# Three homes of expert matrices that cycle to the end of the layer, in a two-layer encoder

## What is computed

```python
D_MODEL = 1024
MOE_EXPERTS = MOE_GROUPS * MOE_EXPERTS_PER_GROUP      # 4 * 8 = 32
MOE_TOP_K = 2
MOE_HIDDEN = D_MODEL // 2
...
    def expert_block(args):
        xb, e = args
        return (jax.nn.silu(xb @ w_gate[e]) * (xb @ w_up[e])) @ w_down[e]
...
    for layer in range(DEPTH):
        ...
        x = x + mix.astype(x.dtype)
        h = rms_norm(x, norm_ffn_g[layer])
        x = x + hier_moe(h, moe_w_group[layer], ..., moe_w_gate[layer], moe_w_up[layer], moe_w_down[layer])
    return rms_norm(x, norm_final_g)
```

## Time and profile before

| what | us, or as said |
|---|---|
| median of 3 runs | 1568.47 (1568.19 to 1569.04) |
| the profiled execution, time | 1564.83 |
| its span, first to last instruction | 1563.0 |
| PE busy / DVE / ACT / POOL | 1389.7 / 531.6 / 244.7 / 194.6 |
| matmuls / weight loads of PE | 7005 / 7005 |
| matrices' queue (q1), share of the 16 DMA engines | 71.9% |
| moved by all DMA engines | 479.25 MB, mean 307 GB/s |
| expert stage of layer 0, first to last gate-and-up product | 344.6 to 805.3 |
| expert stage of layer 1, the same | 1074.9 to 1532.6 |

### The profile page before, as it was taken

The page is one execution under the profiler, slowest core; times in us unless marked ns, Lnnn a source line. Parts: engine busy times, 40 slices in busy tenths (PEclk is TensorE's granted clock), DMA queues, the critical chain, the costliest instruction groups (busy, mean ns, idle before and its releaser), DMA issues. The chain is left out here.

```text
span 1563.0 us, 18994 instructions
## 1 busy us (share of the span) xinstructions
PE 1389.7 (89%) x7005; PEld 660.3 (42%) x7005; DVE 531.6 (34%) x1254; ACT 244.7 (16%) x522; POOL 194.6 (12%) x362
## 2 busy tenths in 40 slices
PE   6999998999988878888889999999998888888786
PEld 3454584454332333333334547865333332333232
DVE  6999986251111111110123156635111111111115
ACT  3211221121000000000011145422000000000002
POOL 5300000011111111111100000001211111111100
PEclk9999999999999999999999999999999999999998
DMA  8313535279999999999996110178899999999996
GB/s 245 129 55 90 67 122 234 116 279 366 409 428 426 428 426 427 425 427 427 426 394 217 55 54 2 57 306 342 362 420 428 427 426 427 428 426 427 426 428 264
DMA packets 76454, 479.25 MB, mean 307 GB/s; under 512 B 16536, under 2 KB 23448, under 8 KB 49776
## 3 DMA queue, kind: packets, MB, share of 16 engines
q1 hardware_dynamic: 63824, 454.36, 71.9%
q0 software_dynamic: 11152, 19.27, 3.4%
q10 hardware_dynamic: 1424, 4.89, 0.8%
HBM read 468.01 MB, written 26.74 MB: 317 GB/s over the span
## 5 line engine op out<-in xcount | busy, mean ns | idle before, releaser
L702 PE MATMUL psum<-ring,work 128*64 128x512 f32 x992 | 474.7, 635 | 76.4 <-DMA ring<-in_moe_w_up 76.4
L703 PE MATMUL psum<-ring,work 128*64 128x512 f32 x992 | 475.3, 636 | 0.0
L702 PEld LDWEIGHTS psum<-ring,work 128*64 128x64 f32 x992 | 139.9, 145 | 382.1 <-issue 316.7
L717 PE MATMUL psum<-ring,work 128*64 128x512 f32 x992 | 226.5, 597 | 48.8 <-DVE work L899 48.6
L896 DVE TENSOR_TENSOR work<-work,psum 64x512 f32<-64x512 f32 x64 | 44.1, 690 | 548.0 <-ACT work L854 547.9
L854 ACT ACTIVATE work<-psum 64x512 f32<-64x512 f32 x64 | 37.8, 590 | 801.2 <-PE psum L703 801.2
L703 PEld LDWEIGHTS psum<-ring,work 128*64 128x64 f32 x992 | 139.9, 145 | 2.0
L717 PEld LDWEIGHTS psum<-ring,work 128*64 128x64 f32 x992 | 72.3, 136 | 161.2 <-issue 156.1
L902 DVE COPY work<-psum 128x512 f32<-128x512 f32 x60 | 41.5, 692 | 236.1 <-PE psum L717 236.1
L1817 PE MATMUL psum<-ring,hT 128*128 128x512 f32 x256 | 112.0, 594 | 0.0
L1098 POOL DMA_INDIRECT work<-h_dram,ints x64 | 66.8, 1044 | 56.9 <-POOL ints L1091 53.1
(11 more groups left out here) (386 smaller groups left out, 1451.7 us busy)
## 6 DMA issues: line engine op xcount, KB each, us to landing
ring<-in_moe_w_down SPq DMA_DIRECT2D x62, 2048.0 KB
ring<-in_moe_w_gate SPq DMA_DIRECT2D x54, 2048.0 KB
ring<-in_moe_w_up SPq DMA_DIRECT2D x54, 2048.0 KB, 22.7
ring<-in_moe_w_gate SPq DMA_DIRECT2D x16, 1024.0 KB
ring<-in_moe_w_up SPq DMA_DIRECT2D x16, 1024.0 KB, 10.1
ring<-in_hyb_w_in SPq DMA_DIRECT2D x5, 2048.0 KB
work<-y_dram SPq DMA_DIRECT2D x16, 512.0 KB, 7.4
ring<-in_swa_w_qkv SPq DMA_DIRECT2D x3, 2048.0 KB
```

Source lines behind the costliest of these rows:

```text
L702: nc.tensor.matmul(bank[2 + b][0:BLK, :], x, g[:, c, :], start=c == 0, stop=c == KC - 1)
L703: i = nc.tensor.matmul(bank[2 + b][BLK:P, :], x, u[:, c, :], start=c == 0, stop=c == KC - 1)
L717: i = nc.tensor.matmul(bank[6 + b][BLK * hf:BLK * (hf + 1), :], HTE[b][:, c, :], d[:, c, hf * HALF:(hf + 1) * HALF], start=c == 0, stop=c ...
```

## The change

Expert e uses home e mod 3 for all e, and its place goes to expert e+3, in both layers. `W2` is thus refilled to the end: with experts 5, 8, ..., 29. SP's calls become one regular sequence (`gate_up` of e, then `rows` of e-1), and the last expert's down matrix waits for down of expert 28 where it waited for that of 29. Because the home and the token buffers repeat together only every six experts, the bodies of PE's and SP's loops hold six steps where they held two; the loops run 4 times where PE's ran 13 and SP's 12 times. PE's experts 5 and 6 are now written out ahead of the loop. `HALVED` has two entries where it had four: only the loads that replace experts 0 and 1 come in halves. Nothing is changed in what ACT, DVE and POOL do.

```diff
+        def weights(home, which):
+
+            return W2[which] if home == 2 else W(3 * home + which)
...
-        HALVED = (0, 1, 3, 4)
+        PER_HOME = [len(range(h, NE, 3)) for h in range(3)]
+
+
+        HALVED = (0, 1)
...
-            step(1, 1)
-            step(2, 0)
-            step(3, 1)
-            step(4, 0)
+            for e in range(1, 5):
+                step(e, e % 2, e)
             pe.wait_ge(g_O.s, 2 * (l + 1))
             pe.sem_inc(passed, 1)
-            with pe.Fori(0, (NE - 6) // 2) as i:
-                step(i * 2 + 5, 1)
-                step(i * 2 + 6, 0)
+            step(5, 1, 5)
+            step(6, 0, 6)
+            with pe.Fori(0, (NE - 8) // 6) as i:
+                for c in range(7, 13):
+                    step(i * 6 + c, c % 2, c, i * 2)
...
-            def gate_up(e, used, par):
+            def gate_up(used, home):
+
                 if isinstance(used, int) and used in HALVED:
                     for h in range(2):
                         sp.wait_ge(e_gu, gu_done(l, used) - 1 + h)
                         for k, v in enumerate((wg_v, wu_v)):
                             cols = slice(2048 * h, 2048 * h + 2048)
...
+                            sp.dma_start(weights(home, k)[:, cols], v[used + 3 + NE * l][:, cols]).then_inc(loaded(home, k), 16)
                     return
                 sp.wait_ge(e_gu, gu_done(l, used))
...
+                for k in range(2):
+                    load_block_w(sp, used + 3 + NE * l, home, k, loaded(home, k))
+
+            def rows(used, home):
+                sp.wait_ge(e_dn, b0 + used + 1)
+                load_block_w(sp, used + 3 + NE * l, home, 2, loaded(home, 2))
+
+            gate_up(0, 0)
+            for e in range(1, 5):
+                gate_up(e, e % 3)
+                rows(e - 1, (e - 1) % 3)
+            with sp.Fori(0, (NE - 8) // 6) as i:
+                for c in range(5, 11):
+                    gate_up(i * 6 + c, c % 3)
+                    rows(i * 6 + (c - 1), (c - 1) % 3)
+            rows(NE - 4, (NE - 4) % 3)
+            sp.wait_ge(e_dn, b0 + NE - 2)
```

More of the change, by code:

```diff
@@ L694, in pe_x, with pe_gu @@
             i.then_inc(done, 1)
-        def pe_gu(pe, b, wait_w, done, w2=False, halves=False):
-            g, u = (shp(w, KC, HID) for w in W2[0:2]) if w2 else (Wrows(3 * b, KC), Wrows(3 * b + 1, KC))
+        def weights(home, which):
+            return W2[which] if home == 2 else W(3 * home + which)
+        def pe_gu(pe, b, wait_w, done, home, halves=False):
+            g, u = (shp(weights(home, k), KC, HID) for k in range(2))
             wait_w(0)
@@ L711, in pe_ht, with pe_dn @@
             i.then_inc(done, 1)
-        def pe_dn(b, done, w2=False):
-            d = shp(W2[2], HC, D) if w2 else Wrows(3 * b + 2, HC)
+        def pe_dn(b, done, home):
+            d = shp(weights(home, 2), HC, D)
             for c in range(HC):
@@ L721, in moe_w_base @@
         def moe_w_base(l, slot):
-            return MIX_LOADS[l][slot] + l * (NE // 2 - (slot < 3) + 2 * (slot % 3 < 2))
-        HALVED = (0, 1, 3, 4)
+            return MIX_LOADS[l][slot] + l * (PER_HOME[0] + (slot % 3 < 2))
+        PER_HOME = [len(range(h, NE, 3)) for h in range(3)]
+        HALVED = (0, 1)
         def gu_done(l, e):
@@ L738, in pe_moe, with step @@
             b0 = NE * l
-            def step(e, par, first=False, last=False):
+            def step(e, par, c, turn=0, first=False, last=False):
                 b, o = par, 1 - par
@@ L749, in step @@
                     pe_ht(o, e_ht)
-                pe_gu(pe, b, lambda k: w_wait(k, e, b), e_gu, w2=is2(e),
+                pe_gu(pe, b, lambda k: w_wait(k, c, turn), e_gu, c % 3,
                       halves=isinstance(e, int) and e in HALVED)
@@ L762, in step, with down, w_wait @@
                 if not first:
-                    down(e, par)
-            def down(e, par):
+                    down(e, par, c - 1, turn)
+            def down(e, par, c, turn=0):
                 o = 1 - par
                 pe.wait_ge(e_he, b0 + e)
-                w_wait(2, e - 1, o)
+                w_wait(2, c, turn)
                 if l or not (isinstance(e, int) and e < 3):
                     pe.wait_ge(e_y, b0 + e - 2)
[L771 to L779, removed]
+                pe_dn(o, e_dn, c % 3)
+            def w_wait(k, c, turn):
+                home, loads = c % 3, (turn + c // 3) * 16 + 16
+                if home == 2:
+                    pe.wait_ge(w2_in[k], loads + 16 * PER_HOME[2] * l)
                     return
[L781 to L784, removed]
+                if k < 2 and not (isinstance(turn, int) and c < 3):
+                    loads = loads + 16
+                pe.wait_ge(w_in[3 * home + k], loads + 16 * moe_w_base(l, 3 * home + k))
             def x_count(e, par):
@@ L811, in pe_moe @@
             pe_keep_busy(6, 512)
-            step(0, 0, first=True)
+            step(0, 0, 0, first=True)
             pe_overflow_lists(pe, l)
-            step(1, 1)
-            step(2, 0)
-            step(3, 1)
-            step(4, 0)
+            for e in range(1, 5):
+                step(e, e % 2, e)
             pe.wait_ge(g_O.s, 2 * (l + 1))
             pe.sem_inc(passed, 1)
-            with pe.Fori(0, (NE - 6) // 2) as i:
-                step(i * 2 + 5, 1)
-                step(i * 2 + 6, 0)
+            step(5, 1, 5)
[3 more added lines that the diff above has]
+                    step(i * 6 + c, c % 2, c, i * 2)
             n = overflow_count(pe, l)
-            step(NE - 1, 1, last=True)
+            step(NE - 1, 1, NE - 1, last=True)
             pe.wait_ge(e_h, b0 + NE)
             pe_ht(1, e_ht)
-            down(NE, 0)
+            down(NE, 0, NE - 1)
             def body(j):
@@ L834, in body @@
                 pe.wait_ge(o["xe"], j + 1)
-                pe_gu(pe, 1, lambda k: pe.wait_ge(o["w"], j * 48 + 48), o["gu"])
+                pe_gu(pe, 1, lambda k: pe.wait_ge(o["w"], j * 48 + 48), o["gu"], 1)
                 pe.wait_ge(o["h"], j + 1)
@@ L840, in body @@
                 pe.wait_ge(e_y, b0 + NE)
-                pe_dn(1, o["dn"])
+                pe_dn(1, o["dn"], 1)
                 pe.wait_ge(o["y"], j + 1)
@@ L991, in load_block_w @@
             v = src[bass.ds(le, 1), :, :].rearrange("a p n -> (a p) n") if not isinstance(le, int) else src[le]
-            q.dma_start(W(3 * b + which), v).then_inc(done, 16)
+            q.dma_start(weights(b, which), v).then_inc(done, 16)
         def sp_moe(sp, l, frees, next_loads):
@@ L1009, in sp_moe, with loaded @@
             sp.dma_start(W2[2], wd_v[b2]).then_inc(w2_in[2], 16)
[L1011 to L1021, removed]
-            def gate_up(e, used, par):
+            def loaded(home, k):
+                return w2_in[k] if home == 2 else w_in[3 * home + k]
+            def gate_up(used, home):
                 if isinstance(used, int) and used in HALVED:
@@ L2158, in pe_mixer1 @@
             hT_ready(pe, 2)
-            base = [16 * (MIX0[i] + NE // 2 - 1 + 2 * (i < 2)) for i in range(3)]
+            base = [16 * moe_w_base(0, i) + 16 * (PER_HOME[0] + (i < 2)) for i in range(3)]
             def queries(i, b):
```

17 lines of the change are left out of this document (removed).

## The result

The changed kernel took 1554.28 us (median of 4 runs, 1552.43 to 1556.55), the kernel before beside it 1568.33 us (4 runs). Two further series of the same kernel gave 1555.27 against 1566.46 us (ratio 0.9927, 0.9905 to 0.995) and 1555.52 against 1565.88 us (0.9929, 0.9908 to 0.9951), so I take 10.4 to 11.2 us as the size of the gain; the first 14 us lie within the same intervals and are partly luck of the draw. The profiled execution took 1556.55 us, span 1554.7, against 1564.83 and 1563.0.

What follows compares the result with a forecast made beforehand. The stream of matrices bounds both expert stages; filling one early hole per layer gives 4.3 us plus 4.9 less 0.6 us, together 8.6 us, all else nothing: 1568.47 - 8.6 = 1559.9 us, range 1556.5 to 1565.0.

Steps and rivals of the forecast that it cites:

- What bounds the kernel: In both expert stages the stream of matrices sets the pace; an early hole costs its full length at the end.
- the signs that I had named: No 2 us window below 300 GB/s; PE's first wait at expert 10 or 11; expert 31 earlier by 4.3 and 8.6 us.
- The hole closes: Early in each stage, earlier issue of expert 5's matrices fills the hole, except 0.6 us in layer 1; together 8.6 us.
- at the rate of the stretch behind: Bytes not moved in the holes, priced at 415 GB/s: 4.3 us in layer 0, 4.9 less 0.6 us in layer 1.
- when it is newly filled: Under the rival that nothing arrives: the stream could run slower early on, 415 against 427 GB/s.
- a little more than the sum, by a better rate with more queued: 427 in place of 415 GB/s for 100 us: 2.8 us a layer, 1554.3 us; chance 0.03.
- My part on a later hole: No second hole in the changed kernel: 5 us in hand at expert 6, cover growing by 2.7 us per expert.
- The longer queue: Rival: matrices wait some 38 us, the scatter takes 2.4 us more, 4.8 us of gain lost; 1564.7 us, chance 0.08.
- The clock: At expert 31 PE's granted clock may flip: 1.7 us per layer, 1558.2 or 1561.6 us with one flipped, chance 0.26.
- The loops of six, home 2, the halves given up: Loops and home 2 in other memory cost nothing; whole loads for experts 5 and 6 only layer 1's 0.6 us.
- Branches that fetch code: Rival: PE's three backward branches per layer fetch their targets; slower from 17.4 us per branch, 1584 us at 20; chance 0.04.
- a gain that doesn't arrive: Rival: PE's tail hangs on something not moving with the stream, or the early rate is lower; 1568.5 us, chance 0.07.

Runs made afterwards that it cites:

- The two experiments with holes: Changed kernel with down of expert 4 put back ahead of gate and up of expert 5: 1562.19 us in both layers, 1559.5 us in layer 1 alone.
- the one with the early down matrix: Changed kernel without SP's wait for the first gathered token block ahead of expert 2's down matrix, both layers: 1568.23 us, ratio 1.0005.

## Why the prediction was right or wrong

**What bounds the kernel: right.** The two experiments with holes show that idle time of the stream early in a stage comes back at the end of the program, 3.7 us for one layer and 6.9 for two. Of the signs that I had named, the deepest window of 2 us in the changed kernel's first trace is at 344 GB/s (not below 300), PE's first wait is at expert 10, and expert 31 starts 6.2 us earlier in layer 0 and 8.6 us earlier in layer 1, where I had 4.3 and 8.6. That the second agrees to the tenth is luck: 5.6 of the 8.6 us were there at the start of layer 1's stage.

**The hole closes: right, at the moments forecast.** Expert 5's gate is issued 0.1 us behind the product of expert 2, at 373.78 (forecast, relative to the start of the stage: 373.6). In layer 1 a part stays, as I wrote: 376 GB/s over 7 us, 0.8 us below 427, where I had charged 0.6; in layer 0, where I had charged nothing, 391 GB/s leave 0.6 us. The worth of what was filled, by the windows of both traces of the kernel before, is 3.6 to 3.9 us in layer 0, (391 - 156 or 173) x 7 / 427, and 3.4 to 4.2 us in layer 1, together 7.0 to 8.1 us. I had 8.6, and the experiment says 6.9: this term was somewhat too large.

**The step that failed: the rate behind the hole.** I priced the hole "at the rate of the stretch behind", 415 GB/s, and noted beside it that the later stage makes 427, as if that were only another price for the same bytes (what 427 GB/s would have moved in the two holes is 8.8 us, not 8.4, with the same 0.6 us off). Later I wrote that the stream is slower "when it is newly filled", a cause that nothing in the rows showed, and as a reason for less gain. The step that failed is that the sum has no term for the stretch behind the hole. The 415 were a mean over smaller holes, such as the 346 GB/s over 4 us above: with two homes the next home comes free only when the queue has nearly run empty. So the deficit itself belonged into the sum, as a term of its own: (427 - 407) x 40 / 427 = 1.9 us in layer 0 and (426 - 410) x 40 / 427 = 1.5 us in layer 1, or 1.4 us in each by the second trace, 2.8 to 3.4 us in all. With it the sum is 9.8 to 11.5 us, and the two later series measured 11.2 and 10.4. The total fits better than its parts: the experiment with the holes put back gives 6.9 us for the holes and 4.3 for the rest, of which PE's start of expert 31 shows 1.5 to 2.5 us, all in layer 0. Where the remainder of the 4.3 us lies stays open. I had named the outcome too, "a little more than the sum, by a better rate with more queued", 2.8 us a layer and 1554.3 us, but gave it a chance of 0.03 and left it out of the range. The first median, 1554.28, meets that figure by luck: the term is about half as large as priced there. The experiment that loads whole matrices with two homes shows such holes at their clearest (338 and 323 GB/s over 8 us), and the one with three homes up to expert 5 shows that filling them needs no more than that. My part on a later hole asked the question for the changed kernel only, and answered it rightly for that. It was not asked of the kernel before.

**In layer 1 the traces show less at PE than in the stream.** From the start of the stage to expert 31, layer 0 gained 5.4 us and layer 1 only 3.0. Where the rest is can be seen behind the start of expert 31, in the windows of the kernel before and then of the changed one, in layer 1:

```profile
1525.53:1534.53 9.00, 9.00 (x43) 3.07 (x44) 1.23 (x3) 0.59 (x1) 1.16 (x2) 1.00 0.87 367
```

```profile
1516.95:1525.95 9.00, 9.00 (x42) 3.65 (x44) 1.03 (x2) 0.59 (x1) 1.16 (x2) 1.00 0.68 285
```

In the 9 us from there the changed kernel moves (367 - 285) x 9 = 0.74 MB less, so that much more of the last two down matrices, which nobody waits for yet, had been moved when expert 31 could start: 1.7 us of stream. The other traces have it too (366 GB/s in the second of the kernel before, 259 and 295 in those of the changed one). It brings no time at the end in this pair of traces: from the start of expert 31 in layer 1 to the end of the span it is 37.5 us before and 37.8 us after. The longer queue isn't the cause, since the kernel with three homes up to expert 5 alone has 279 GB/s there. What is stays open.

**The clock: mechanism right, and the side it falls on is chance.** In layer 0 expert 31's product took 8.74 us before and 7.05 us now, in layer 1 7.08 and 7.05. In the second trace of the changed kernel both were slow (8.65 and 8.75 us, with a granted clock of 0.82 and 0.81 over 9 us), and that execution was the longest of its series, 1559.89 us. So this term belongs to the single execution and not to the change. It is part of the scatter of both kernels.

**The loops of six, home 2, the halves given up: nothing, as forecast.** There are 41 code transfers where 35 were. I had said four more; six steps of PE per layer are written out anew (experts 5 and 6, and four more in the body), and 6 x 2 x 112 instructions of 66 bytes are 89 KB or 5.4 transfers. The kernel with loops of two steps and only experts 5 and 6 written out has 37, as the same count has it. So the body of 44 KB was fetched once and its three backward branches fetched nothing. The branch behind expert 12 costs nothing in layer 0: expert 13 starts 15.25 us behind expert 12, the pace of the stream. By the Trainium skill (Runtime: NRT & Kernel Launch, section Instruction fetch mechanics) a branch to code outside the current window of two pages has to fetch its target first; this count and this pace show no such fetch on PE.

**The rivals.** The longer queue is as long as I had worked out, and harms nobody. The DMA view of the changed kernel, 600 to 700 us, answers the earlier trace rows:

```profile
ring<-in_moe_w_up SPq DMA_DIRECT2D x5, 2048.0 KB, 36.7
...
y_dram<-work,ints POOLq DMA_INDIRECT x7, 8.0
```

Matrices take 36.7 us to land (38 forecast), and the scatter still 8.0 us, not the 10.4 of my slope of 0.16 us per us. The slope was drawn through two points that differed in more than the queue's length: the first lies in the stretch with the smaller holes. Branches that fetch code, and a gain that doesn't arrive, were not seen.

**The range.** It ended at 1556.5, "the flipped clock and 1.7 us more". With the term of the small holes it would have ended near 1553.5. The median of 1554.28 is 5.6 us below the forecast; the larger gain is 1.8 to 2.6 of these (10.4 to 11.2 in place of 8.6), and the rest is scatter from series to series: in the three later ones the kernel before is 1.6 to 2.5 us below its 1568.33, and the changed one 1.0 to 1.2 us above its 1554.28.

## What to carry to other kernels

Where a stream of transfers is the bound, take its best sustained rate as the measure and sum up everything below it, however shallow: a stretch at 96% of the rate for 40 us is a hole of 1.6 us that no single window shows. Ask of each refill how much is still queued when its place comes free; two buffers per stream can be too few just where the consumer is still faster than the stream, and one more refill of a third one is then enough. A stream that is kept idle for a small transfer that all else waits for may be idle for a good reason: measure before filling it.

## What the hardware showed beyond that

A gather of one token block took 3.0 us to be of use on a nearly idle stream, and 6.9 us (8.5 in layer 1) while the stream moved 2 to 3 MB, although it is on another queue. PE, idle meanwhile, then lost a further 1.3 us per layer at the lower clock, and the whole made the program 12 to 13 us longer. The scatter, in contrast, took 8.0 us whether the matrices' queue was 22.9 us or 36.7 us long: by these rows it matters whether the transfer engines are busy, and not how much is queued.

The runs of one kernel scatter by different amounts. Of the kernels with 12 runs each, the kernel before ranged over 7.9 us, the changed one with the holes put back over 8.2 us, the one with two entries of HALVED and two homes over 11.9 us, and the one with the early down matrix, which has no holes, over 5.5 us. Why a stream with holes should scatter more stays open.
